# The last group of rows: added in PSUM by a slot-by-token table, and the final norm's products on two engines

## What is computed

```python
def rms_norm(x, g):
    xf = x.astype(jnp.float32)
    y = xf * lax.rsqrt(jnp.mean(xf * xf, axis=-1, keepdims=True) + RMS_EPS)
    return (y * g.astype(jnp.float32)).astype(x.dtype)
...
    down = lax.ragged_dot(clamped_swiglu(up), w_down, group_sizes) + b_down[e_sorted]
    out = jnp.zeros_like(hf).at[tok].add(down * g_sorted[:, None].astype(down.dtype))
    return out.reshape(B, S, D)
...
        h = rms_norm(x, g_pre_ffn[l]) * (1 + sc_f) + sh_f
        y = moe(h, w_router[l], b_router[l], w_up[l], b_up[l], w_down[l], b_down[l])
        x = x + gt_f * rms_norm(y, g_post_ffn[l])
```

## Time and profile before

| | |
|---|---|
| median of 3 runs | 1455.89 us (1455.56 to 1461.43) |
| the profiled execution | 1458.35 us |
| its span, first to last instruction | 1456.4 us |
| mean granted clock of TensorE | 0.966 of 2.4 GHz |
| TensorE busy with matmuls | 1306.2 us, 90% |
| VectorE, ScalarE, GpSimd busy | 629.9, 345.4 and 309.4 us |
| share of the chain of waits | TensorE 62%, DMA 30%, VectorE 5% |

### The profile page before, as it was taken

How to read it: one execution, slowest core, us unless ns; L and a number is a source line. 1 busy time by engine, 2 the same in 40 slices (tenths; PEclk the granted TensorE clock), 3 DMA queues, 4 the chain that set the end, 5 groups by cost and what they waited for, 6 DMA issues and landing times.

```text
span 1456.4 us, 45667 instructions
## 1 busy us (share of the span) xinstructions
PE 1306.2 (90%) x18550; PEld 763.2 (52%) x18551; DVE 629.9 (43%) x1679; ACT 345.4 (24%) x844; POOL 309.4 (21%) x420
## 2 busy tenths in 40 slices
PE   5999999999979999887989978799999999898992
PEld 2464555665546555554545534455555555554551
DVE  2558546786465344333324322333334333333334
ACT  2120005665221222111212211122222222221222
POOL 0400002444001222221212211122222222221220
PEclk9999999999978999999999989999999999999996
DMA  9758404001879999999999999999989889999996
GB/s 352 266 202 290 155 0 174 2 2 53 353 276 385 384 398 414 424 423 418 420 423 396 402 425 425 418 407 399 419 337 420 360 353 398 419 425 419 396 419 240
DMA packets 70095, 483.93 MB, mean 332 GB/s; under 512 B 10488, under 2 KB 17164, under 8 KB 45480
## 3 DMA queue, kind: packets, MB, share of 16 engines
q1 hardware_dynamic: 61536, 465.52, 77.6%
q0 software_dynamic: 8240, 17.85, 4.7%
q10 hardware_dynamic: 280, 0.02, 0.0%
HBM read 467.87 MB, written 20.06 MB: 335 GB/s over the span
## 4 chain that ended last, share of the span: by engine, by line
PE 62%; DMA 30%; DVE 5%; issue 2%; SPq 1%; POOL 0%; ACT 0%; ACTq 0%; POOLq 0%; DVEq 0%
DMA arena<-in_w_down 26%; PE ps L1916 24%; PE ps L1936 14%; PE ps L1563 7%; PE ps L1820 4%; DMA arena<-in_w_in 2%; PE ps L1678 2%; PE ps L1711 2%; PE ps L1751 1%; PE ps L1530 1%; PE ps L1924 1%; DVE arena L952 1%; DVE arena L1150 1%; DMA arena<-in_w_ada 1%; PE ps L1737 1%
## 5 line engine op out<-in xcount | busy, mean ns | idle before, releaser
L1916 PE MATMUL ps<-arena 128*32 128x256 f32 x10240 | 584.3, 382 | 44.1 <-issue 29.6
L1916 PEld LDWEIGHTS ps<-arena 128*32 128x32 f32 x10240 | 340.9, 111 | 264.3 <-issue 54.0
L1936 PE MATMUL ps<-arena 128*32 128x256 f32 x5120 | 307.3, 391 | 42.8 <-DMA arena<-in_w_down 42.6
L1399 DVE TENSOR_SCALAR arena<-ps 128x128 f32<-128x128 f32 x160 | 46.6, 291 | 579.8 <-PE ps L1924 574.2
L1936 PEld LDWEIGHTS ps<-arena 128*32 128x32 f32 x5120 | 156.7, 111 | 169.4 <-issue 56.4
L868 ACT ACTIVATE arena<-ps,arena 32x256 f32<-32x256 f32 x320 | 149.2, 466 | 337.0 <-PE ps L1936 291.6
L643 POOL DMA_INDIRECT arena<-xn_rows,arena x83 | 86.1, 1037 | 468.9 <-DVE arena L1367 240.5
L635 POOL DMA_INDIRECT token_sums<-arena x81 | 112.2, 1385 | 219.6 <-ACT arena L868 216.6
L862 ACT ACTIVATE arena<-arena 128x128 f32<-128x128 f32 x160 | 49.6, 310 | 447.6 <-DVE arena L1399 447.6
L1563 PE MATMUL ps<-arena 128*128 128x512 f32 (+1 forms) x320 | 129.7, 561 | 3.1 <-DMA arena<-in_w_in 3.1
L618 POOL TENSOR_SCALAR arena<-arena 128x128 f32<-128x128 f32 (+3 forms) x48 | 51.7, 1082 | 220.3 <-DVE arena L1164 199.2
(11 more groups left out here) (325 smaller groups left out, 971.0 us busy)
## 6 DMA issues: line engine op xcount, KB each, us to landing
arena<-in_w_up SPq DMA_DIRECT2D x128, 2048.0 KB, 21.3
arena<-in_w_down SPq DMA_DIRECT2D x64, 2048.0 KB, 28.5
arena<-in_w_ada SPq DMA_DIRECT2D x12, 2048.0 KB, 11.7
arena<-in_w_in SPq DMA_DIRECT2D x5, 2048.0 KB, 10.8
arena<-in_w_o SPq DMA_DIRECT2D x2, 2048.0 KB, 11.3
arena<-in_x SPq DMA_DIRECT2D x4, 512.0 KB, 5.2
arena<-in_w_cmp_v SPq DMA_DIRECT2D x2, 1024.0 KB, 12.9
arena<-in_w_cmp_k SPq DMA_DIRECT2D x1, 2048.0 KB, 10.7
```

Source lines behind the costliest of these rows:

```text
L1916: ins = pe.matmul(out_of(y, g), xgT[:, 2 * n + k, :], tiles[par][n][:, k, at:at + 256], start=(n == 0 and k == 0), stop=False)
L1936: ins = pe.matmul(out_of(5, g), actT[:, y, k, :], tiles[par][4 + y][:, k, 256 * g:256 * (g + 1)], start=False, stop=(y == 1 and k == 3))
```

## The change

The last group (c = total - 1) no longer goes through memory.

- The loops of GpSimd and ScalarE run over total - 1 groups. The last group's two sigmoids are still ScalarE's, so the pair of sigmoids moves to the end of the loop's body, with one pair ahead of it; the order of the instructions stays.
- VectorE makes a table `last_slots`: partition 32g + s, column t, is 1 where row s of the last group belongs to token t. It needs the token numbers 0 to 511 on 32 partitions (`token_row`, a constant loaded by SyncE) and the tokens of the group (`last_row`). A row of the group that is empty has a number outside, and gives zeros. Then VectorE scales the down result with the gates into `last_y`.
- TensorE multiplies table and rows: for each of the four token tiles and each quarter one matmul with 32 rows, 128 tokens and 256 columns. The four of a tile have different row groups and different banks.
- VectorE adds each tile's PSUM result to `acc_in`, which SyncE loads once the scatter of the group before the last has landed. ScalarE squares the sums.
- The products with `gbf_fin` are GpSimd's for tiles 0, 1 and 2 and VectorE's for tile 3. There is one root and one refinement for all four tiles.
- SyncE's order of loads is now token numbers, sums, norm's weights, and the residual in four parts in the order 0, 1, 3, 2 (`FIN_ORDER`), in which the results are made and written too.

```diff
+    tokens = nc.inline_tensor(np.tile(np.arange(SEQ, dtype=np.float32), (SLOTS, 1)), name="token_numbers").ap()
...
+        last_slots, last_y = take(FIN_AT + 3 * TILE + D, SEQ), take(FIN_AT + 3 * TILE + D + SEQ, D // 4)
+        token_row = take(FIN_AT + 3 * TILE + 2 * D, SEQ, parts=SLOTS)
+        last_row = take(FIN_AT + 3 * TILE + 3 * D, 1, parts=SLOTS)
+        y_ps = [ps[:, i // 2:8:2, 256 * (i % 2):256 * (i % 2) + 256] for i in range(NT)]
+        FIN_ORDER = (0, 1, 3, 2)
+
+        def by_quarter(row):
+            return row.rearrange("p (g n) -> p g n", g=4)
...
             sp.wait_ge(gbf_out, 16)
             total = of_place(FIRST, N_PART, N_PART, MAX_CH - 3)
             sp.wait_ge(tile_used[5], of_place(FIRST, N_PART - 1, N_PART - 1, MAX_CH - 4))
+            sp.dma_start(token_row, tokens).then_inc(filled, 16)
+            sp.wait_ge(written, (total - 1) * 16 + FILLED)
+            for i in range(NT):
+                sp.dma_start(acc_in[:, i, :], acc_d[P * i:P * (i + 1)]).then_inc(fin_in[i], 16)
             sp.dma_start(gbf_fin, gbf_d).then_inc(x2_back, 16)
-            sp.dma_start(x2fin, x2_d.rearrange("(i p) n -> p i n", p=P)).then_inc(x2_back, 16)
-            sp.wait_ge(written, total * 16 + FILLED)
-            for i in range(NT):
-                sp.dma_start(acc_in[:, i, :], acc_d[P * i:P * (i + 1)])\
-                  .then_inc(fin_in[i], 16)
-            for i in range(NT):
-                sp.wait_ge(fin_dve, i + 1)
+            for i in FIN_ORDER:
+                sp.dma_start(x2fin[:, i, :], x2_d[P * i:P * (i + 1)]).then_inc(x2_in[i], 16)
+            for n, i in enumerate(FIN_ORDER):
+                sp.wait_ge(fin_dve, n + 1)
                 sp.dma_start(out[i * P:(i + 1) * P, :], result[:, i, :]).then_inc(out_done, 16)
...
             pool.wait_ge(idx_ready, 3)
-            with pool.Fori(0, total) as c:
+            with pool.Fori(0, total - 1) as c:
...
                 add_rows(c)
+
+            pool.wait_ge(x2_back, 16)
+            for i in range(NT - 1):
+                pool.wait_ge(row_sums, i + 1)
+                pool.tensor_tensor(gained_y[:, i, :], acc_in[:, i, :], gbf_fin, ALU.mult).then_inc(gain_ready, 1)
...
-            with act_e.Fori(0, total) as c:
+
+            def sigmoids(c):
                 for y in range(2):
                     act_e.wait_ge(glu_ready, c * 2 + y + 1)
                     act_e.activation(sw_s[:, y], sw_g[:, y], ACT.Sigmoid, scale=ALPHA).then_inc(sig_ready, 1)
+
+            sigmoids(0)
+            with act_e.Fori(0, total - 1) as c:
                 act_e.wait_ge(tile_used[5], c + 1)
                 act_e.wait_ge(written, c * 16 + FILLED)
                 act_e.sem_inc(act_turn, 1)
@@ -868,22 +889,14 @@
                     ins = act_e.activation(ybuf[:, 256 * g:256 * (g + 1)], ps[rows, 5, 0:256], ACT.Copy,
                                            scale=gate_all[rows, bass.ds(c, 1)])
                 ins.then_inc(y_ready, 1)
+                sigmoids(c + 1)
             act_e.activation(fin[:, 16:17], gk[:, 0, 0:1], ACT.Sqrt)
...
-            def tail_square(i):
-                act_e.wait_ge(fin_in[i], 16)
+            for i in range(NT):
+                act_e.wait_ge(row_sums, i + 1)
                 act_e.activation(squared, acc_in[:, i, :], ACT.Square, accum_out=fin[:, i:i + 1]).then_inc(sumsq, 1)
...
-            def tail_root(k, lo, hi):
-                act_e.wait_ge(ms_ready, NORM_ALL + k)
-                act_e.activation(fin[:, 8 + lo:8 + hi], fin[:, 4 + lo:4 + hi], ACT.Sqrt).then_inc(root_ready, 1)
-
-            for i in range(NT - 1):
-                tail_square(i)
-            tail_root(1, 0, NT - 1)
-            tail_square(NT - 1)
-            tail_root(2, NT - 1, NT)
+            act_e.wait_ge(ms_ready, NORM_ALL + 1)
+            act_e.activation(fin[:, 8:12], fin[:, 4:8], ACT.Sqrt).then_inc(root_ready, 1)
...
-            v.wait_ge(x2_back, 32)
-
-            def gained(i):
+            v.wait_ge(filled, 48)
+            tstep(v.tensor_copy(last_row, row_all[:, bass.ds(total - 1, 1)]))
+            for g in range(4):
+                v.tensor_scalar(last_slots[SLOTS * g:SLOTS * (g + 1)], token_row, last_row, None, ALU.is_equal)
+            v.wait_ge(gate_sb, 1)
+            v.wait_ge(tile_used[5], total)
+            v.tensor_scalar(last_y, ps[:, 5, 0:256], gate_all[:, bass.ds(total - 1, 1)], None, ALU.mult).then_inc(last_out, 1)
+
+            v.wait_ge(y_tail, 4)
+            for i in range(NT):
                 v.wait_ge(fin_in[i], 16)
-                return v.tensor_tensor(gained_y[:, i, :], acc_in[:, i, :], gbf_fin, ALU.mult)
-
...
-                v.wait_ge(root_ready, NORM_ALL + k)
-                tstep(v.reciprocal(r, r))
-                tstep(v.tensor_tensor(t, r, r, ALU.mult))
-                tstep(v.tensor_tensor(t, t, ms, ALU.mult))
-                tstep(v.tensor_scalar(t, t, -0.5, 1.5, ALU.mult, ALU.add))
-                tstep(v.tensor_tensor(r, r, t, ALU.mult))
-
-            def mean_square(lo, hi):
-                v.tensor_scalar(fin[:, 4 + lo:4 + hi], fin[:, lo:hi], 1.0 / D, EPS, ALU.mult, ALU.add).then_inc(ms_ready, 1)
-
-            def finish(i):
-                v.scalar_tensor_tensor(out=result[:, i, :], in0=gained_y[:, i, :], scalar=fin[:, 8 + i:9 + i],
+                row = by_quarter(acc_in[:, i, :])
+                v.tensor_tensor(row, y_ps[i], row, ALU.add).then_inc(row_sums, 1)
+            v.wait_ge(x2_back, 16)
+            v.wait_ge(row_sums, NT)
+            tstep(v.tensor_tensor(gained_y[:, NT - 1, :], acc_in[:, NT - 1, :], gbf_fin, ALU.mult))
+            v.wait_ge(sumsq, SQ_ALL + NT)
+            ms, r, half = [fin[:, at:at + NT] for at in (4, 8, 12)]
+            v.tensor_scalar(ms, fin[:, 0:NT], 1.0 / D, EPS, ALU.mult, ALU.add).then_inc(ms_ready, 1)
+            v.wait_ge(root_ready, NORM_ALL + 1)
+            tstep(v.reciprocal(r, r))
+            tstep(v.tensor_tensor(half, r, r, ALU.mult))
+            tstep(v.tensor_tensor(half, half, ms, ALU.mult))
+            tstep(v.tensor_scalar(half, half, -0.5, 1.5, ALU.mult, ALU.add))
+            tstep(v.tensor_tensor(r, r, half, ALU.mult))
+            for i in FIN_ORDER:
+                if i < NT - 1:
+                    v.wait_ge(gain_ready, i + 1)
+                v.wait_ge(x2_in[i], 16)
+                v.scalar_tensor_tensor(out=result[:, i, :], in0=gained_y[:, i, :], scalar=r[:, i:i + 1],
                                        in1=x2fin[:, i, :], op0=ALU.mult, op1=ALU.add).then_inc(fin_dve, 1)
-
-            last = NT - 1
-            for i in range(last - 1):
-                gained(i)
-            ins = gained(last - 1)
-            v.wait_ge(sumsq, SQ_ALL + last)
-            tstep(ins)
-            mean_square(0, last)
-            tstep(gained(last))
-            final_rstd(1, 0, last)
-            for i in range(last):
-                finish(i)
-            v.wait_ge(sumsq, SQ_ALL + NT)
-            mean_square(last, NT)
-            final_rstd(2, last, NT)
-            finish(last)
 
...
+            pe.wait_ge(gate_sb, 1)
+            pe.wait_ge(idx_ready, 3)
+            pe.wait_ge(last_out, 1)
+            for i in range(NT):
+                for g in range(4):
+                    rows = slice(SLOTS * g, SLOTS * (g + 1))
+                    ins = pe.matmul(y_ps[i][:, g, :], last_slots[rows, P * i:P * (i + 1)], last_y[rows, :],
+                                    start=True, stop=True)
+                    if i == NT - 1:
+                        ins.then_inc(y_tail, 1)
```

6 lines of the change are left out of this document (3 added, 3 removed).

## The result

The kernel after the change takes 1453.97 us (median of 22 runs, 1449.6 to 1459.89); the kernel before, on the same chips, 1457.73 us (22 runs, 1454.53 to 1463.07). The ratio is 0.9972 with a 95% interval of 0.9962 to 0.9982: 0.28% or some 4 us less. The forecast was 1452.3 us, 3.6 less than before, and "within 0.5%". The 1.7 us by which the time itself is off belong to the kernel before, whose median went from 1455.89 (3 runs) to 1457.73 with more runs.

What follows compares the result with a forecast made beforehand. The prediction took the last w_down load as the bound, leaving a 26.5 us end to shorten. Its terms ended the span at 1452.8 instead of 1456.4, 3.6 us less: 1455.89 - 3.6 = 1452.3 us, range 1448.5 to 1457.0.

Steps and rivals of the forecast that it cites:

- Part 1: Last group's round through memory goes; sum tiles follow the weights, landing 1428.6 to 1433.0, gain_row 1434.3; none asked for earlier.
- Part 2: VectorE's table, one copy and four comparisons, 1427.3 to 1429.4, inside the wait for the last matmuls, costing nothing.
- Part 3: Scaling the last group on VectorE: one operation from PSUM, 0.43 us, in place of four of ScalarE.
- Part 4: Sixteen new TensorE matmuls, four row groups together, 3.6 us at the low clock; 1.8 us at full clock.
- second rival: Tail matmuls: row groups take turns, 32 records cost 13.8 us instead of 3.6; total 1462.4 us; chance 0.08.
- Part 5: VectorE sums, 1.224 us each; shared products, 2.4 us on GpSimd; the engines hold each other; final sums begin at 1444.2.
- third rival: VectorE's sums are held beside GpSimd too, alternating with products; 1455.7 us, so the change brings nothing; chance 0.12.
- first rival: VectorE's product and the root's correction run beside GpSimd's products without holding; 1449.9 us; chance 0.20.
- Part 6: The end: four final sums in 4.96 us, last write 3.44 us plus 0.2 allowed; span ends at 1452.8.

Runs made afterwards that it cites:

- one_gp: Changed kernel with only tile 0's product on GpSimd and the other three on VectorE; 1455.02 us, ratio to the kernel before 0.9959 to 0.9986.
- halves: Changed kernel with the tail's matmuls in two halves of PSUM banks, first two sums waiting for eight matmuls; 1455.23 us, ratio to before 0.9967 to 0.9997.
- serial_rows: Changed kernel with the sixteen tail matmuls ordered by row group instead of by tile; 1456.64 us (1 run).
- combined: Changed kernel with one product on GpSimd, mean's step on ScalarE, gain_row loaded before the sums, matmuls in two bank halves; 1451.27 us, ratio to before 0.9956.
- all_dve: Changed kernel with all four products on VectorE and none on GpSimd; 1454.24 us, ratio to the kernel before 0.9953 to 0.9979.
- mean_on_act: Changed kernel with the mean square's step on ScalarE instead of VectorE; 1456.51 us, ratio to the kernel before 0.9960 to 0.9986.
- gain_first: Changed kernel with gain_row loaded ahead of the sums' tiles; 1454.65 us, ratio to the kernel before 0.9969.

## Why the prediction was right, step by step

The 3.6 us less (3.8 in the medians, 4.2 between the two profiled tails) and "within 0.5%" came out. In the total this was in part luck, as the end of this section says. The tail's terms, in us:

| | forecast | after |
|---|---|---|
| end of experts to first new matmul | 0.6 | 0.88 |
| to the first sum | 3.65 | 2.13 |
| first sum to first final sum | 10.1 | 10.72 |
| four final sums and the last write | 8.6 | 8.66 |
| tail | 22.9 | 22.4 |

**Part 1** was right: the tiles came in the order of the queue, all before the sums asked for them; gain_row was the close one. After had it 1.1 us ahead of GpSimd's question, where the prediction said 1.2. That "no product asks earlier" fails where the experts' last matmuls run at the full clock: in one_gp it was 1.6 us late, in halves more.

**Part 2** was right. The numbers landed just behind the last weights, the table was ready 1.0 us before the matmuls ended. In one_gp, halves and serial_rows those ended sooner, and scaling began 0.40 us behind them instead of 0.25: the table was late, by 0.15 us.

**Part 3**: 0.48 us instead of 0.43. The term lacked the ways around it: 0.25 us from the last matmul to VectorE and 0.15 back, so 0.88 and not 0.6.

**Part 4** was right in its mechanism (four row groups together, eight steps of four records) and mis-sized in the state of the clock: 2.01 us against 3.6. The bound "at full clock 1.8" was named, the clock's return by 1431.7 too; it came back already before the part. Where it stays low, the part takes 3.80 us, close to the forecast. The 13.8 us for 32 records one behind another, over 3.80, are a factor of 3.6. The Trainium skill (TensorE: Matmul & The Clock Gate, Measured speedup vs the span model) has 3.07 for four row groups; the measurement decides. For the price of the second rival the prediction took one record after another; serial_rows, the nearest to it, still ran two groups at a time.

**Part 5, the sums**: 1.215 us each and 4.62 for four, also beside GpSimd: the third rival is out. The 1.224 counted each start anew; in a row a sum adds 1.14.

**Part 5, the products**: 2.35 us, forecast 2.4. VectorE's held product, 2.42 us, ended 1.1 us behind GpSimd's second, as forecast; the third one lasted 3.32 us, forecast 3.25 (1440.3 to 1443.55). The first rival, in which they don't meet, is out; in combined they don't meet, because GpSimd has only one. The sentence that sums the prediction up gives the hold 5 us; by its own first rival it was 2.4 (1452.3 against 1449.9), and in after it is 3.2 (10.72 against the 7.5 of all_dve's arithmetic). The same sentence has 14.5 us up to the old tiles' arrival; the one that the chain waited for came after 13.1.

**The step that failed** is "the mean square and the root go on meanwhile (one input each), but the first step of the root's correction multiplies two SBUF inputs and waits". The mean's step has one input and was held, 2.19 us, to the end of the third product. So mean, root and reciprocal came behind the hold, not beside it. GpSimd's third product ended 9.34 us behind the first sum (forecast 9.45); from there to the final sums it is 1.38 us instead of the forecast 0.65. mean_on_act takes the step away and has 0.66 (1445.66 to 1446.32). The rule that I had read out of the earlier trace rows, two inputs from SBUF, was too narrow, and the trace of before had the row against it (timeline):

```profile
65.07 1.45 POOL L600 TENSOR_SCALAR arena<-arena 128x384 bf16<-128x384 f32 x1
...
66.16 0.40 DVE L996 TENSOR_SCALAR arena<-arena 128x32 f32<-128x32 f32 x1
```

L996 has one input; it took 0.18 us at 63.41 and 0.40 here, to 0.04 us behind the end of GpSimd's. The Trainium skill's section (SBUF — State Buffer, SBUF: two separate sides) names two kinds of VectorE operation that take the lock against GpSimd, those with two SBUF inputs and those in a two-port performance mode; the prediction had used the first alone. The trace agrees as far as it goes: the products, with two SBUF inputs, are held, and so is the multiply-add of 128x4, though no row tells in which mode it ran; the sums with one input from PSUM and RECIPROCAL aren't.

**Part 6** was right: 4.87 us for the final sums, 3.8 behind them to the end.

Two errors had opposite signs: 1.5 us less by the clock in Part 4, and 0.9 more, 0.3 in Part 3 and 0.6 by the mean's step. That made the total look better than its parts. With the clock that the forecast had assumed, as in five of the nine profiles, the changed kernel's tail is 24.1 us (gain_first) and not 22.9; that 22.4 came so near is in part the luck of the profiled execution.

## What to carry to other kernels

Work handed to GpSimd is worth what it takes from VectorE less what the two then hold each other: here three of four products brought 0.2 us, and one of four 0.7 (10.91 to 10.21), although gain_row was late for it. Keep small steps that lead to another engine (a mean before a root) off the engine that can be held. When a wait in front of an engine gets shorter, look again at every load that was just in time: gain_row had 1.1 us to spare in after; in halves it was 3.9 us late, 0.9 of them by the shorter stretch and the rest by the execution, so that the shorter stretch mostly lengthened a wait.

## What the runs showed of the hardware

- A VectorE operation on four columns, with one input from SBUF, can be held as long as GpSimd's product runs (the mean's step, 2.19 us instead of 0.17); RECIPROCAL on the same four columns isn't (0.18 at 1440.43 in halves, beside GpSimd's product), nor is a sum with one input from PSUM (1.215 us).
- Sixteen matmuls on four row groups take 2.01 us at the full clock when neighbours in the program's order are on different groups. Ordered by group they took 7.22 us, two thirds of it at the low clock, some 4.9 at the full one by estimate, with two groups at a time.
- TensorE's clock, once at 0.50, was back after 3.4 us in one execution (after) and still low after 9 in another (all_dve), with the same work on TensorE up to there. It fell with TensorE waiting in both, and with TensorE busy in serial_rows (1430.4). It is worth 1.8 us of the tail.
